# Experts of a mixture layer sorted by their row count on the chip, and four of sixteen pairs cut 96 to 32

## The reference

```
g_logits = (hf @ w_rg + b_rg);  pg_top, g_idx = top_k(softmax(g_logits), 1)
e_logits = (hf @ w_re + b_re).reshape(-1, N_GROUPS, EXPERTS_PER_GROUP)
pe_top, j_idx = top_k(softmax(e_logits of the group g_idx), 2)
weights = pg_top * pe_top / sum(pe_top)
e_idx = g_idx * 8 + j_idx
for e in range(32):
    act = silu(hf @ w_gate[e]) * (hf @ w_up[e])
    y = y + combine[:, e:e+1] * (act @ w_down[e])
```

## Time and profile before

| | |
|---|---|
| median of three runs | 1674.65 us |
| the profiled execution's own time | 1674.94 us |
| its span in the trace | 1673.1 us |
| PE busy | 1575.4 us, 94% of the span |
| DVE busy | 824.9 us, 49% |
| moved by DMA | 260.41 MB, mean 156 GB/s |
| start of the first `gate_up` | 1407.20 us |
| span from there to the end | 265.9 us |

### The profile page before, as it was taken

The page is one execution under the profiler, slowest core; times in us unless marked ns, Lnnn a source line. Parts: engine busy times, 40 slices in busy tenths (PEclk is TensorE's granted clock), DMA queues, the critical chain, the costliest instruction groups (busy, mean ns, idle before and its releaser), DMA issues.

```text
span 1673.1 us, 19707 instructions
## 1 busy us (share of the span) xinstructions
PE 1575.4 (94%) x8009; PEld 1185.0 (71%) x8009; DVE 824.9 (49%) x1442; ACT 542.5 (32%) x881; POOL 84.2 (5%) x106
## 2 busy tenths in 40 slices
PE   8999999999999999999999899999999996888876
PEld 6987777777787788888887688787678884333332
DVE  6556334355364776666223874436663736222211
ACT  5334444344433322222113433332354323111110
POOL 5000000000000000000000010000000001121111
PEclk9999999999999999999999899999999997999998
DMA  5335212212333465565323132312213467999995
GB/s 166 114 101 133 71 52 75 63 64 76 76 101 101 151 196 187 190 207 176 101 101 98 51 102 83 94 51 76 69 58 134 158 238 299 399 411 403 404 408 187
DMA packets 147070, 260.41 MB, mean 156 GB/s; under 512 B 16568, under 2 KB 121316, under 8 KB 133664
## 3 DMA queue, kind: packets, MB, share of 16 engines
q1 hardware_dynamic: 138544, 241.41, 41.1%
q0 software_dynamic: 8432, 17.70, 3.7%
HBM read 253.79 MB, written 15.25 MB: 161 GB/s over the span
## 4 chain that ended last, share of the span: by engine, by line
PE 83%; DVE 8%; issue 4%; ACT 2%; DMA 1%; POOL 0%; POOLq 0%; DVEq 0%; ACTq 0%
PE psum L2499 20%; PE psum L2500 20%; PE psum L2501 20%; PE psum L3080 6%; PE psum L3097 4%; PE psum L2810 1%; PE psum L2799 1%; PE psum L2782 1%; DVE cst L2013 1%; DVE WL L1561 1%; PE psum L3058 1%; PE psum L2704 1%; ACT Sb L1115 1%; DMA Xg<-h_rows,tok 1%; PE psum L2566 1%
## 5 line engine op out<-in xcount | busy, mean ns | idle before, releaser
L2499 PE MATMUL psum<-AHs,WH 128*128 128x512 f32 x744 | 306.8, 412 | 7.5 <-DVE WL L1561 4.6
L1561 DVE TENSOR_TENSOR WL<-raw,WH 128x2048 fp32r<-128x2048 f32 (+1 forms) x100 | 226.7, 2267 | 175.5 <-ACT WH L1030 175.0
L2500 PE MATMUL psum<-ALs,WH 128*128 128x512 f32 x744 | 293.6, 395 | 0.0
L2501 PE MATMUL psum<-AHs,WL 128*128 128x512 f32 x744 | 293.4, 394 | 0.0
L1030 ACT ACTIVATE WH<-raw 128x2048 fp32r<-128x2048 f32 (+1 forms) x100 | 189.0, 1890 | 128.8 <-PE psum L2501 99.3
L2499 PEld LDWEIGHTS psum<-AHs,WH 128*128 128x128 f32 x744 | 142.0, 191 | 45.0 <-DVE ALs L1749 5.8
L2499 PE MATMUL psum<-AH,WH 128*128 128x512 f32 (+1 forms) x464 | 169.0, 364 | 0.0
L2500 PEld LDWEIGHTS psum<-ALs,WH 128*128 128x128 f32 x744 | 142.0, 191 | 31.0 <-issue 3.1
L2500 PE MATMUL psum<-AL,WH 128*128 128x512 f32 (+1 forms) x464 | 163.9, 353 | 0.0
L2501 PEld LDWEIGHTS psum<-AHs,WL 128*128 128x128 f32 x744 | 141.8, 191 | 31.0
L2501 PE MATMUL psum<-AH,WL 128*128 128x512 f32 (+1 forms) x464 | 163.1, 352 | 0.0
(11 more groups left out here) (561 smaller groups left out, 2276.6 us busy)
## 6 DMA issues: line engine op xcount, KB each, us to landing
raw<-w_in SPq DMA_DIRECT2D x45, 1024.0 KB, 5.2
WE<-w_gate SPq DMA_DIRECT2D x34, 1024.0 KB, 21.0
WE<-w_up SPq DMA_DIRECT2D x34, 1024.0 KB, 24.6
WE<-w_down SPq DMA_DIRECT2D x34, 1024.0 KB, 19.8
araw<-w_ada SPq DMA_DIRECT2D x24, 1024.0 KB, 5.6
raw<-w_ffn_in SPq DMA_DIRECT2D x22, 1024.0 KB, 7.8
raw<-w_ffn_out SPq DMA_DIRECT2D x11, 1024.0 KB, 4.8
raw<-w_out SPq DMA_DIRECT2D x8, 1024.0 KB, 5.1
```

What stands on the lines that cost most here:

```text
L1561: V.tensor_tensor(WL[:, n, 0:w], raw[:, n, 0:w], WH[:, fed[0] % HL, 0:w].bitcast(F32), ALU.subtract).then_inc(S_("lo_ready"), 1)
L2499: MM(dst, lh, rh, start=first, stop=False)
L2500: MM(dst, lh, rl, start=False, stop=False)
L2501: return MM(dst, ll, rh, start=False, stop=last)
```

## The change

There is no overflow pair. Of each side's 16 experts the last three (13 to 15 and 29 to 31) are held at pairs 0 to 2, since their weights are loaded before the choice of experts is known. The other 13 of each side are sorted on DVE by their row count: those of the first side from large to small, those of the second from small to large, so that the largest meets the smallest. The sorted numbers go to the tile `order`, from which SP reads the two expert numbers of each of the pairs 3 to 15. In pairs 3 and 4 the first expert has 96 rows and the second 32; in pairs 14 and 15 the first has 32 and the second 96. In these four pairs each matmul of the experts is cut into four parts of 32 rows (`parts_of`). There are 16 pairs and 32 expert loads. The conditional part runs if any expert has more rows than its place, and then runs 15 pairs of one expert each. The work that fills the token lists moves on DVE and PE: the rows and places of all sorted experts are worked out beside the first two pairs, not ahead of the first. The diff, cut to its core:

```
-BASE = NE // 2 + 1
-NPAIR = BASE + NOV - 2
-OVER = 3
+BASE = NE // 2
+NPAIR = BASE + NOV
+HELD = 3
+SORTED = NE // 2 - HELD
+WIDE = 2
...
+        def parts_of(t):
+            if t >= BASE:
+                return [(0, CAP, 0)]
+            if HELD <= t < HELD + WIDE:
+                return [(0, 32, 0), (32, 64, 0), (64, 96, 0), (96, 128, 1)]
+            if t >= BASE - WIDE:
+                return [(0, 32, 0), (32, 64, 1), (64, 96, 1), (96, 128, 1)]
+            return [(0, 64, 0), (64, 128, 1)]
...
-            return eng.value_load(eover[0:1, NOV:NOV + 1], min_val=0, max_val=NOV) > 2
+            return eng.value_load(eover[0:1, NOV:NOV + 1], min_val=0, max_val=NOV) > 0
...
-            sp.wait_ge(*when("overflow_ready", 1))
-            over = [sp.value_load(eover[0:1, x:x + 1], min_val=0, max_val=NE - 1) for x in range(2)]
+            sp.wait_ge(*when("order_ready", 1))
             sp.wait_ge(*when("out_set", 16 * 3))
-            load_pair(sp, OVER, over)
-            for t in range(OVER + 1, BASE):
-                x = t - 1
-                load_pair(sp, t, (x + NE // 2, x) if x % 2 else (x, x + NE // 2))
+            for t in range(HELD, BASE):
+                load_pair(sp, t, [sp.value_load(order[0:1, x:x + 1], min_val=0, max_val=NE - 1)
+                                  for x in (t - HELD, SORTED + t - HELD)])
...
-                for half in range(2 if t == OVER else 1):
-                    if half:
-                        pool.wait_ge(*when(f"y_stored{t % 2}", y_stores(t) - 16))
...
-            pool.wait_ge(*when("over_tokens", 1))
             for t in range(BASE):
+                if t + 2 == HELD:
+                    pool.wait_ge(*when("over_tokens", 1))
                 if t + 2 < BASE:
                     gather(t + 2)
                 scatter(t)
...
             link(V.tensor_copy(cnt, count))
-            full_blocks(over, cnt, thr[:, 0, :], steps7[0])
-            link(V.memset(base_, 1.0))
-            link(V.tensor_tensor_scan(incl, base_, over, 0.0, ALU.mult, ALU.add))
-            link(V.tensor_tensor(base_, incl, over, ALU.subtract))
             dve.wait_ge(*when("base_used", 1))
-            token_of(tok, 5).then_inc(S_("tokens_ready"), 1)
+            token_of(tok[:, 0:HELD], 5, HELD).then_inc(S_("tokens_ready"), 1)
...
+            def sorted_places():
+                key = movable(incl)
+                link(V.scalar_tensor_tensor(incl, cnt, float(NE), K("expert"), ALU.mult, ALU.subtract))
+                link(V.tensor_tensor(versus, key.unsqueeze(2).to_broadcast(sides), key.unsqueeze(3).to_broadcast(sides), ALU.is_ge))
+                link(V.tensor_reduce(movable(wider), versus, AX_X, ALU.add))
...
+                V.tensor_copy(order, named).then_inc(S_("order_ready"), 1)
...
             def pairs(t0, t1):
                 xt_copy(t0)
                 if t0 == 0:
-                    overflow_numbers()
-                    overflow_tokens()
-                    token_weights()
+                    widths()
                 for t in range(t0, t1):
                     gated(t)
+                    if t == 1:
+                        overflow_tokens()
+                        weights_by_row()
+                        y_scaled(0)
+                        overflow_numbers()
                     if t + 1 < t1:
                         xt_copy(t + 1)
                     if t == 0:
-                        weights_by_row()
+                        rows_and_pairs()
+                        token_weights()
+                        continue
                     y_scaled(t)
...
                 for k in range(KC):
-                    for half in halves(t):
-                        rows = slice(CAP * half, CAP * half + CAP)
-                        ins = MM(bank(3)[rows], XT[:, t % 2, P * k + CAP * half:P * k + CAP * half + CAP],
+                    for lo, hi, half in parts_of(t):
+                        ins = MM(bank(3)[lo:hi], XT[:, t % 2, P * k + lo:P * k + hi],
                                  GU[gate_up_slot(t, half)].rearrange("p (g k n) -> p k g n", g=2, k=KC)[:, k],
                                  start=k == 0, stop=k == KC - 1)
...
                 transpose_rows(t0)
-                if t0 == 0:
-                    overflow_spots()
                 for t in range(t0, t1):
                     gate_up(t)
+                    if t == 1:
+                        overflow_spots()
+                        weights_by_row()
```

More of the change, by code:

```diff
@@ L811, in y_stores, with held @@
         def y_stores(t):
-            return 16 * (t // 2 + 1 + (t >= OVER and t % 2 == OVER % 2))
+            return 16 * (t // 2 + 1)
+        def held(t, half):
+            return NE // 2 * half + SORTED + t
+        def parts_of(t):
[6 more added lines that the diff above has]
+            return [(0, 64, 0), (64, 128, 1)]
         choice_gap, choice_exp, weight1, weight2 = (r4[:, n, :] for n in (0, 1, 2, 3))
@@ L970, in scatter @@
                     pool.wait_ge(*when("out_set", 16 * 3))
-                if t == OVER:
-                    pool.wait_ge(*when("tokover_ready", 1))
-                for half in range(2 if t == OVER else 1):
-                    if half:
-                        pool.wait_ge(*when(f"y_stored{t % 2}", y_stores(t) - 16))
[L976 to L979, removed]
+                pool.indirect_dma_start(out=out[0], out_offset=bass.IndirectOffsetOnAxis(ap=rows_of_pair(t), axis=0),
+                                        in_=Yt[:, t % 2, :], in_offset=None, bounds_check=S - 1, oob_is_err=False,
+                                        compute_op=ALU.add).then_inc(S_(f"y_stored{t % 2}"), 16)
             def out_columns(c0, c1):
@@ L2342, in rows_with, with pairs_with, token_of @@
                                        row.unsqueeze(2).to_broadcast([P, 2 * NB, P]), ALU.is_equal)
[L2344 to L2355, removed]
+            def pairs_with(n, pair, count):
+                shape = [P, 2 * NB, count]
+                wider_ = [P, 2 * NB, 2, count]
+                link(V.tensor_tensor(here[:, :, 0:count], K("expert", count).unsqueeze(1).to_broadcast(shape),
+                                     pair.unsqueeze(2).to_broadcast(shape), ALU.is_equal))
+                return V.tensor_tensor(inpair[n], here[:, :, 0:count].unsqueeze(2).to_broadcast(wider_),
+                                       ids.unsqueeze(3).to_broadcast(wider_), ALU.mult)
+            def token_of(dst, b, count):
+                found = bank(b, 2 * count).rearrange("p (c n) -> p c n", c=2)
+                link(V.tensor_scalar(spot[:, 0:count], found[:, 0, :], NOBODY, None, ALU.add))
+                return V.tensor_tensor(dst, spot[:, 0:count], found[:, 1, :], ALU.add)
             by_tile = [r8[:, n] for n in range(9)]
[L2358 removed]
+            rkh, rk, home, pair, bs, blk, ov_, cap_, row_ = [x.rearrange("p c t -> p (c t)") for x in by_tile]
+            extra, past = (r8[:, n].rearrange("p c t -> p (c t)") for n in (11, 12))
             chosen(by_tile[3], places[:, 1, :].unsqueeze(1).unsqueeze(1), prod[0])
[L2360 removed]
+            link(pairs_with(0, pair, HELD))
             dve.wait_ge(*when("rank_mm", 1))
@@ new lines, in widths @@
+            def widths():
+                link(V.tensor_scalar(wider, places[:, 1, :], HELD - 0.5, None, ALU.is_ge))
+                link(V.scalar_tensor_tensor(wider, places[:, 1, :], HELD + WIDE - 0.5, wider, ALU.is_ge, ALU.subtract))
+                link(V.scalar_tensor_tensor(wider, places[:, 1, :], BASE - WIDE - 0.5, wider, ALU.is_ge, ALU.add))
+                for side in range(2):
+                    half = slice(NE // 2 * side, NE // 2 * side + NE // 2)
+                    link(V.tensor_scalar(cap[:, half], wider[:, half], 64.0 * side - 32.0, float(CAP), ALU.mult, ALU.add))
+                link(V.tensor_tensor(cnt, cnt, cap, ALU.subtract))
+                full_blocks(over, cnt, thr[:, 0, :], steps7[0])
+                link(V.memset(base_, 1.0))
+                link(V.tensor_tensor_scan(incl, base_, over, 0.0, ALU.mult, ALU.add))
+                link(V.tensor_tensor(base_, incl, over, ALU.subtract))
+                for n, x in ((2, places[:, 0, :]), (3, places[:, 1, :]), (4, base_), (7, cap)):
+                    chosen(by_tile[n], x.unsqueeze(1).unsqueeze(1), prod[1])
@@ L3093, in down @@
                     for j in range(2):
-                        for half in halves(t):
-                            rows = slice(CAP * half, CAP * half + CAP)
+                        for lo, hi, half in parts_of(t):
                             o = 2 * DE * KC + D * j + 512 * n
-                            ins = MM(bank(4 + n)[rows], AT[:, t % 2, P * j + CAP * half:P * j + CAP * half + CAP],
+                            ins = MM(bank(4 + n)[lo:hi], AT[:, t % 2, P * j + lo:P * j + hi],
                                      WE[(2 * t + half) % SLOTS][:, o:o + 512], start=j == 0, stop=j == 1)
```

115 lines of the change are left out of this document (65 added, 50 removed).

## The result

The changed kernel takes 1664.91 us (median of 6 runs, 1663.94 to 1669.37) against 1674.87 us of the kernel before on the same chip (6 runs, 1673.67 to 1675.97): a ratio of 0.9946, 95% interval 0.9934 to 0.9958. It is faster, by 10.0 us and not by 16.1; 1658.5 had been forecast, in 1654 to 1664.

What follows compares the result with a forecast made beforehand. DMA transfers were taken to bound the expert stage. The terms -16.3 - 1.0 + 0.2 + 0 + 0 + 1.0 = -16.1 us gave 1658.8 us profiled and 1658.5 us median, range 1654 to 1664, chance 0.78.

Steps and rivals of the forecast that it cites:

- What bounds the kernel: Expert stage: DMAs bound it at about 405 GB/s; its end is stream start plus bytes plus a PE tail of 24.8 us.
- SP's register loads: Two more ahead of each of pairs 4 to 15, about 1 us a pair, covered by queued loads: 0.
- One pair less: Expert weight stream: six loads, 6.29 MB, go, with one gather and two scatters: -16.3 us, between -15.5 and -17.15.
- The stream starts earlier: First token list: five DVE overflow operations move behind it, so the whole stream moves: -1.0 us, between 0 and -1.5.
- Four parts of 32 rows: Four uneven pairs on PE: four tiles run at once, only later starts inside rounds are added: +0.2 us.
- A: Rival, uneven pairs: parts take turns two at a time, 10.52 us more on PE each; 1681 us; chance 0.04.
- B: Rival, uneven pairs: parts overlap in part, 3.5 us a pair, only the last pair's in the tail; 1662 us; chance 0.08.
- What moves in the first pairs: DVE, PE and POOL work moved into the first pairs: PE may wait 2 to 3 us at pair 3; 0, at most +1.5.
- The tail's clock: Last pair on PE: waits for weights cost clock and slow some operations: +1.0 us, between 0 and +3.4.
- C: Rival, weight stream: SP's register loads or early waits let transfers run dry; 1661 to 1671 us; chance 0.07.
- D: Rival, conditional part: an expert does not fit its place, 15 pairs of one expert run; 1864 us; chance 0.02.
- a sign of being wrong: Uneven `gate_up` over 8 us at full clock, DMA share below 1 between pairs 4 and 14, or over 32 experts loaded.

## Why the prediction was right or wrong

*What bounds the kernel*: right. The transfers set the stage's end, PE's late gather and SP's register loads cost nothing that shows.

*One pair less*: this is the step that failed. Its sentence "The token rows stay 1024 gathered and 1024 added, so by bytes alone it is 15.5 us" counted the bytes and not where they lie. Taking out the alternation was in the diff beside the pair, and the prediction put it at nothing. It costs 4.5 to 4.8 us: 4.5 is an estimate, the 11 rows that the fullest engine gains (73 to 84) at 0.41 us, and 4.8 is what the kernel before lost without its alternation. (The changed sides give back more, 242.7 - 237.4 = 5.3 us, but they take 13 rows away.) The pair's own price of 16.3 was probably too high as well. The mean rate of 405 GB/s includes the gathers and scatters, which stay; in a stretch at its best before's rate is 426, and 6.29 MB at 426 is 14.8; the weights' own share gives 15.0 and the run with half a pair 14.5, which alone would not rule out 16.3. That something came back for the index lists that went, for which the prediction added 0.8, no run shows. Together -14.5 + 4.8 = -9.7 to -15.0 + 4.5 = -10.5, where the means of two profiles give 242.7 - 252.0 = -9.3. That this closes so well is partly luck, since each interval wanders by 2 to 3 us.

*The stream starts earlier*: right, -1.1 against -1.0; SP's down load follows `spot` 5.2 us later as before (5.1).

*Four parts of 32 rows*: right, 0.13 us in pair 3 and 0.01 in the last pair, so A and B are false: 64 records in 7.00 us against 32 in 6.87, and in 7.11 against 7.10. The +3.2 that the prediction drew from the Trainium skill, "TensorE: Matmul & The Clock Gate", section "Measured speedup vs the span model", is not what this trace shows.

*SP's register loads*: right. *What moves in the first pairs*: nearly right. PE waits 3.46 us at pair 3, a little longer than the 2 to 3 foreseen (the gather, issued right behind the first scatter, takes 11.66 us and not 9.57), still under the transfers.

*The tail's clock*: +0.1 and not +1.0; the last pair ran at the full clock here (granted 1.00). In other profiles it did not (8.61 us with the sides changed, granted 0.57), so the term is a chance and not a size.

*Rivals*: C's range held the time, but not its mechanism: the constants on SP change nothing. D did not come. None of the rivals was the one that decided. Nor did a sign of being wrong show: 96 loads, an uneven `gate_up` of 7.00, a mean share of 1.01 from 1405 to 1625. What failed lay behind 1625, where the prediction looked only at the start of the last `gate_up` (1637 and not 1631).

The median: -9.3 - 1.1 + 0.1 = -10.3 from the profiles, -10.0 from the runs.

With the sides of three pairs changed over, the kernel beats both: 1656.19 and 1658.84 us.

## What to carry to other kernels

Where transfers are the bound, count what each DMA engine moves and not only the sum: a transfer that spreads over all engines is complete when the fullest one is, and a share that falls to a half or a quarter ahead of the end can mean that only so many still have work. A line that looks like bookkeeping (which half an expert lies in, how rows are spread over partitions) can be what keeps the engines even; when a change drops it, price it. And price a load by what its own packets take or by the best rate of the stream, not by a mean that holds gathers too.

## What the runs showed of the hardware

The DMA share at the end of the stream agrees with a count of the engines that still have work: 0.51 with rows heaped on 64 partitions, 0.26 with rows heaped on the first places of each 32. With the same bytes, the order of the rows on the partitions alone moved the time by 24 us (1682.62 against 1658.84). Four fp32 tiles of 32 columns, three of them with the same moving data, ran in one round of 0.43 us.
